# Rows of 309 words instead of 304 under the moving operands of an MLA + mLSTM layer on one Trainium2 core

## The chip, the cores and the metric

One NeuronCore of one Trainium2 chip runs the whole kernel. The metric is the device time of one execution in microseconds. TensorE multiplies matrices, VectorE (DVE), ScalarE (ACT) and GpSimd (POOL) do the rest, and SyncE (SP) issues nearly all loads of weights.

## The reference

One layer of a streaming encoder, for 256 prompt frames, 32 frames of a running stream and 16 learned meta tokens: 304 token columns in all, model width 4096. Cut to what matters here:

```
h = rmsnorm(x) * gain                              # 304 tokens x 4096
p = h @ w_in                                       # latents, mLSTM q, k, v, gates
q = rmsnorm(cq) @ w_q_up ; kv = ckv @ w_kv_up      # cq: 1536 wide, ckv: 512 wide
a = attention(q, kv, kpe) * silu(za)               # 16 heads x 128
m = sigmoid(mo) * rmsnorm(mlstm(q, k, v)) * silu(zb)   # 4 heads x 512
y = x + concat([a, m]) @ w_out                     # 4096 x 4096
```

All inputs and outputs are float32.

## The kernel before

A float32 product is made of three products in the rounded type float32r. Activations and weights are each split into a high part and the remainder, and one 128x128 block of weights times one 128-row block of activations is three matmuls of helper `mm3`: high weights by high activations (L1678), high weights by low activations (L1681), low weights by high activations (L1682). The weights are the stationary operand (128 columns of `whi` or `wlo`), the activations the moving one (`xhi` or `xlo`, 288 or 304 token columns). The result adds up in a PSUM bank over the 32 blocks of the model width.

`group` is the loop of every large projection: for each of the 32 blocks k ("a unit"), for each of four column tiles ct, one `mm3`, so 12 matmuls to a unit. A unit's weights come by DMA as a 128x512 block into `raw`, ScalarE rounds them to `whi` (L727), VectorE takes the remainder to `wlo` (L1132); both have four slots, so the two engines may run three units ahead. `unit_used` counts units that TensorE is done with, and ScalarE waits for it before it overwrites a slot.

The activations stay in SBUF from beginning to end. `xhi` and `xlo` are tiles of 128 partitions by 32 rows of 304 words, one row to each k. The gated mix for the output projection is written over them: before the change, as `mhi` and `mlo`, 32 rows of 288 words that begin where `xhi` and `xlo` begin. Row t of `mhi` is written by ScalarE (`mix`, line 1081) once `unit_used` shows that unit t of the last gate projection is done; VectorE writes `mlo` (line 1622) after it. The latents have tiles of the same sort: `cqhi`, `cqlo` (12 rows of 288 words), `ckhi`, `cklo` (4 rows of 432 words), and are the moving operand of the query and key projections. In the value projection `whi` moves and `ckhi` is stationary.

Where a row begins follows from the sizes of the tiles, which are laid out one behind the other, each start at a multiple of 32 bytes. Counted in bytes modulo 256, the first column that a matmul reads lies here ("place"; for `xhi` with 288 columns it is column 16, with 304 columns it is column 0):

```
tile          start  row step   places of its rows, k = 0, 1, 2, ...   how many
xhi, xlo       192     192      0, 192, 128, 64, 0, ...                  4
mhi, mlo       192     128      192, 64, 192, ...                        2
cqhi, cqlo     192     128      192, 64, 192, ...                        2
ckhi, cklo     192     192      192, 128, 64, 0                          4
whi, wlo       128       0      128 in every slot (512 bytes per column tile)
```

All these are multiples of 64. Small float32r operands lie elsewhere: the rows of `sqr` and `rsr` (squares, high and low parts) begin at place 32 or 160, half way between two multiples of 64; with 288 words they are multiplied by `ones_r` or `blockones_r` in lines 1762, 1858 and 1859. The rows of `ksh`, line 1761, begin at 192 or 64. The plain float32 operand `mqT` of line 2026 begins at 96 or 32.

The program order on each engine is the order of the code; the engines meet at semaphores, and the waits are on constants that `use` works out from a table of phases.

Of the kernel before, what the change touches and what calls it, by code (L numbers as in the profile page):

```python
# [8 lines left out]
SEQ, DEC, PAST, N_META = 256, 32, 128, 16  # L9
# [19 lines left out]
P = 128  # L29
NT = N_META + SEQ + DEC  # L30
NQ = SEQ + DEC
NKV = NT + PAST
C_SAMPLE = N_META + SEQ
KT = D_MODEL // P
KQ = Q_LORA // P
KC = KV_LORA // P
# [13 lines left out]
QT = [(0, 128), (128, 128), (256, 32)]  # L50

MQT = [(0, 112), (112, 128), (240, 48)]

MLW = [(0, 288), (288, 176), (464, 48)]
LAST = NT - 64
# [24 lines left out]
U_OUT = U_GATE + 12 * KT  # L80
# [30 lines left out]
def y_banks(g):  # L111

    return f"out{g}", 4 * (g % 2)
# [14 lines left out]
def use(phase, bank, nth=0, i=0):  # L128

    before, uses = BASE[phase]  # L130
    return before[bank] + nth + i * uses[bank]
# [8 lines left out]
CONST_AT = {}  # L140
# [59 lines left out]
def hymba_step(nc, x_prompt, x_sample, cache_ckv, cache_kpe, state_C, state_n, state_m, meta, norm_gain,  # L200
# [3 lines left out]
    f32, f32r = mybir.dt.float32, mybir.dt.float32r  # L204
# [4 lines left out]
    with ctx:  # L209
        def keep(stack):  # L210
            return lambda name, shape, dt=f32: stack.enter_context(nc.sbuf_tensor(name, shape, dt))

        def sem(name):
            return ctx.enter_context(nc.semaphore(name))
# [6 lines left out]
        con = sb("con", [P, CONST_COLS])  # L221
# [21 lines left out]


        px = ExitStack()
        xhi = keep(px)("xhi", [P, KT, NT], f32r)
        xlo = keep(px)("xlo", [P, KT, NT], f32r)


        p1 = ExitStack()  # L250
# [3 lines left out]

        p2 = ExitStack()
        sb2 = keep(p2)
        cqhi = sb2("cqhi", [P, KQ, NQ], f32r)
        cqlo = sb2("cqlo", [P, KQ, NQ], f32r)
        ckhi = sb2("ckhi", [P, KC, NKV], f32r)
        cklo = sb2("cklo", [P, KC, NKV], f32r)  # L260
        kpe2 = [sb2(f"kpe{h}", [P, NKX]) for h in range(2)]
        qn_ = sb2("qn", [P, SEQ + NQ + WIDE])
        qn = qn_[:, 0:2 * NQ].rearrange("p (h n) -> p h n", h=2)
# [48 lines left out]
        p3 = ExitStack()  # L312
        sb3 = keep(p3)
        hT = sb3("hT", [P, 16, NQ])
        mask = sb3("mask", [P, 512])
        kwh = sb3("kwh", [P, 4, DQK], f32r)
        kwl = sb3("kwl", [P, 2, DQK], f32r)
        vth = sb3("vth", [P, 3, DV], f32r)
# [42 lines left out]
        xres = keep(p4)("xres", [P, 3, 512])  # L361
        p4.close()
        px.close()
        p5 = ExitStack()
        mhi = keep(p5)("mhi", [P, KT, NQ], f32r)
        keep(p5)("meta_gap", [P, KT * N_META])
        mlo = keep(p5)("mlo", [P, KT, NQ], f32r)
        p5.close()

        bank = [ctx.enter_context(nc.psum_tensor(f"bank{b}", [P, 512], f32)) for b in range(8)]  # L370
        full = [sem(f"bank{b}_full") for b in range(8)]
# [47 lines left out]
        mix_hi, mix_lo = sem("mix_hi"), sem("mix_lo")  # L419
# [13 lines left out]
        def _(sp):  # L433
# [36 lines left out]
            for n in range(KT // 2):  # L470
                for b, (a, _) in enumerate(X_BLOCKS):
                    if a == 2 * n * P:
                        x_block(b)
                first_weights(n)
# [231 lines left out]
        def _(act):  # L706
# [265 lines left out]
            def row_hooks(k):  # L972
                if k == 4:

                    act.wait_ge(free[5], use("rows", 5) + 1)
                    act.wait_ge(ml_zero, 1)
                    R = rows
                    nc.scalar.activation(R["mrow"][:, 0:NT], R["xf"][:, 0:NT], ACT.Abs).then_inc(r_abs, 1)
                    act.wait_ge(r_abs, 1)
                    nc.scalar.activation(R["mrow"][:, 0:NT], R["mrow"][:, 0:NT], ACT.Exp, scale=-1.0).then_inc(r_e, 1)  # L980
                    act.wait_ge(r_e, 1)
                    nc.scalar.activation(R["mrow"][:, 0:NT], R["mrow"][:, 0:NT], ACT.Ln, bias=1.0).then_inc(r_l, 1)
                if k == 12:
                    act.wait_ge(r_v, 11)
                    act.wait_ge(full[7], use("rows", 7) + 1)
                    for t, (_, n) in enumerate(MQT):
                        nc.scalar.activation(emcol[0:n, t, :], bank[7][0:n, 4 * t:4 * t + 4], ACT.Exp,
                                             scale=-1.0).then_inc(free[7] if t == 2 else r_em, 1)
# [3 lines left out]
            def mlstm(phase, i, h):  # L992

                def hooks(k):
# [31 lines left out]
                    if k == 17:  # L1026
                        act.wait_ge(din_d, h + 1)
                        for t, (_, n) in enumerate(MQT):
                            b = 5 + t
# [643 lines left out]
        def _(pe):  # L1673
            mm, tr = nc.tensor.matmul, nc.tensor.transpose

            def mm3(out, w_hi, w_lo, m_hi, m_lo, start, stop, opens=False, **kw):

                ins = mm(out, w_hi, m_hi, start=start, stop=False, **kw)  # L1678
                if opens:
                    ins.then_inc(unit_used, 1)  # L1680
                mm(out, w_hi, m_lo, start=False, stop=False, **kw)  # L1681
                return mm(out, w_lo, m_hi, start=False, stop=stop, **kw)  # L1682
# [5 lines left out]
            def fill(phase, b, nth=0, i=0):  # L1688

                before = use(phase, b, nth, i)  # L1690
                if not (isinstance(before, int) and before == 0):
                    pe.wait_ge(free[b], before)
# [12 lines left out]
                ins.then_inc(full[b], 1)  # L1705

            def group(u, phase, nth, i, c0, hooks=lambda k: None, a_hi=xhi, a_lo=xlo, ready=None, x_ready=False,
                      queries=0, b0=0, turn=(0, 2, 1, 3)):

                n = NT - c0  # L1710
                for k in range(KT):
                    pe.wait_ge(lo_done, u + k + 1)
                    if ready is not None:
                        pe.wait_ge(ready, k + 1)
                    if x_ready:
                        pe.wait_ge(free[4 + k % 4], use("x", 4 + k % 4, k // 4) + 1)
                    for ct in range(4) if k else turn:
                        if k == 0:
                            fill(phase, b0 + ct, nth, i)
                        s = slice(ct * P, ct * P + P)  # L1720
                        skip = N_META if ct < queries else 0
                        mc = slice(0, NQ) if a_hi is mhi else slice(c0 + skip, NT)
                        ins = mm3(bank[b0 + ct][:, skip:n], whi[:, k % HL_SLOTS, s], wlo[:, k % HL_SLOTS, s],
                                  a_hi[:, k, mc], a_lo[:, k, mc], k == 0, k == KT - 1, k == 0 and ct == 0)
                        if k == KT - 1:
                            ins.then_inc(full[b0 + ct], 1)
                    if k < KT - 1:
                        ins.then_inc(unit_used, 1)
                    hooks(k)
# [8 lines left out]
            for k in range(X_AHEAD):  # L1738
                x_tile(k)
            warm(WARM[1])  # L1740
            group(0, "cq", 0, 0, N_META, lambda k: x_tile(k + X_AHEAD) if k + X_AHEAD < KT else None, x_ready=True)
            def row_sums(k):
                if k == 6:
# [5 lines left out]
                    ins.then_inc(full[4], 1)  # L1749

            group(KT, "cq", 0, 1, N_META)
            group(2 * KT, "cq", 0, 2, N_META, row_sums)

            def cq_squares(k):
# [221 lines left out]
            def row_hooks(k):  # L1976
# [5 lines left out]
                if k == 9:  # L1982
# [7 lines left out]
                    fill("rows", 7)  # L1990
                    for t, (q0, n) in enumerate(MQT):
                        ins = tr(bank[7][0:n, 4 * t:4 * t + WIDE], rows_["mrow"][0:WIDE, N_META + q0:N_META + q0 + n],
# [4 lines left out]
            def mlstm(phase, i, h):  # L1997
# [3 lines left out]
                def hooks(k):  # L2001
# [36 lines left out]
                    if k == 13:  # L2038
# [8 lines left out]
                        pe.wait_ge(C0_in, 16 * (h + 1))  # L2047
                        for q, (q0, m) in enumerate(MQT):
                            b = 5 + q
# [14 lines left out]
                    if k in (14, 15):  # L2064
                        if k == 14:
                            fill(phase, 4, 2, i)
                        for q, (q0, m) in enumerate(MQT):
                            if (q == 2) != (k == 15):
# [11 lines left out]
                    if k == 23:  # L2080
# [3 lines left out]
                        for e in range(4):  # L2084
                            b = 4 + e
                            fill(phase, b, (3, 2, 3, 3)[e], i)
                            for q, (q0, _) in enumerate(MQT):
                                n = asks[q]
# [43 lines left out]
                group(U_GATE + 2 * KT + g * (2 * KT), "gates", 0, g, N_META)  # L2132

            group(U_GATE + 11 * KT, "gate11", 0, 0, N_META, b0=4)
            group(U_OUT, "out0", 0, 0, N_META, a_hi=mhi, a_lo=mlo, ready=mix_lo)

            def y_rows(g):
                phase, b0 = f"out{g + 1}", y_banks(g)[1]
                for b in range(b0, b0 + 4):
                    pe.wait_ge(free[b], use(phase, b))  # L2140
                for t, (q0, m) in enumerate(QT):
                    for ct in range(4):
                        ins = tr(bank[b0 + t][0:m, ct * P:ct * P + P], yT[:, ct, q0:q0 + m], ident)  # L2143
                    ins.then_inc(full[b0 + t], 1)

            for g in range(1, 8):
                group(U_OUT + g * KT, f"out{g}", 0, 0, N_META, lambda k: y_rows(g - 1) if k == 2 else None,
                      a_hi=mhi, a_lo=mlo, b0=y_banks(g)[1])
            for ct in range(4):
                pe.wait_ge(free[4 + ct], use("out7", 4 + ct) + 1)  # L2150
                for t, (q0, m) in enumerate(QT):
# [168 lines left out]
```

## Time and profile before

| | |
|---|---|
| runs (3) | 2059.68, 2059.81, 2060.38 us; median 2059.81 |
| profiled execution, span from first to last instruction | 2057.9 us |
| TensorE busy | 2046.7 us, 99% |
| VectorE, ScalarE, GpSimd busy | 54%, 44%, 9% |
| HBM traffic | 323.28 MB, 157 GB/s over the span |

For the profiled execution the page gives its span and no other time; the median of the runs is 1.9 us longer than that span. TensorE's matmuls overlap each other in the records, so its busy share says only that it never stood still; how fast it went must be read from the distance between the starts of matmuls. One record of a 288-column float32r matmul lasts about 295 ns, but the next one starts about 133 ns after it.

### The profile page before, as it was taken

Reading aid. Unit: us, or ns where it says so; the run is one execution under the profiler, and the core shown is the slowest. Engines: PE = TensorE matmul, PEld = TensorE weight load, DVE = VectorE, ACT = ScalarE, POOL = GpSimd, SP = SyncE. Lnnn points to the kernel's source line nnn. Section 1 sums busy time; section 2 is a strip of 40 time slices with the busy share of each in tenths; the row PEclk is TensorE's granted clock in tenths of the full one; section 3 lists DMA queues with packets and bytes.
Section 4 is the critical chain, followed back from the end, with each engine's and each line's share of the span. In section 5 each row is a group of like instructions: output and inputs, shape, how many; then the busy total and the mean of one; then the engine's idle time right before and its main releaser. Section 6 shows DMA issues by size and latency. Waiting matters only on the chain.

```text
span 2057.9 us, 36249 instructions
## 1 busy us (share of the span) xinstructions
PE 2046.7 (99%) x15059; PEld 2016.6 (98%) x15059; DVE 1110.8 (54%) x1995; ACT 913.7 (44%) x1826; POOL 180.8 (9%) x206
## 2 busy tenths in 40 slices
PE   9999999999999999999999999999999999999999
PEld 9999999999999999999999999999999999999999
DVE  5545767676555445455555555444555654444444
ACT  5644455565444334343444444444444543333333
POOL 0001033333200000000001011000000000000000
PEclk9999999999999999999999999999999999999999
DMA  9655433333454454645445555555555555555554
GB/s 253 178 171 154 118 118 107 101 100 114 124 170 143 145 163 124 174 123 173 137 142 166 166 169 165 165 167 166 169 164 164 164 185 181 185 187 187 186 182 133
DMA packets 197436, 323.28 MB, mean 157 GB/s; under 512 B 21392, under 2 KB 68136, under 8 KB 197272
## 3 DMA queue, kind: packets, MB, share of 16 engines
q1 hardware_dynamic: 195160, 317.45, 52.1%
q10 hardware_dynamic: 2112, 3.51, 0.5%
q8 instruction: 119, 1.95, 0.4%
q14 instruction: 45, 0.37, 0.1%
HBM read 310.11 MB, written 9.62 MB: 155 GB/s over the span
## 4 chain that ended last, share of the span: by engine, by line
PE 96%; ACT 2%; DVE 1%; issue 1%; DMA 0%; DVEq 0%; ACTq 0%
PE bank L1678 29%; PE bank L1682 29%; PE bank L1681 29%; PE bank L1941 1%; PE bank L1843 1%; PE bank L1840 1%; PE bank L1842 1%; PE bank L1906 1%; PE bank L1907 1%; ACT whi L727 0%; PE bank L2143 0%; PE bank L1703 0%; ACT rsb L819 0%; PE bank L2026 0%; ACT rsb L817 0%
## 5 line engine op out<-in xcount | busy, mean ns | idle before, releaser
L1132 DVE TENSOR_TENSOR wlo<-raw,whi 128x512 fp32r<-128x512 f32 (+1 forms) x1256 | 820.0, 662 | 885.5 <-ACT whi L727 881.9
L727 ACT CAST whi<-raw 128x512 fp32r<-128x512 f32 (+1 forms) x1256 | 708.7, 577 | 980.5 <-PE bank L1682 945.7
L1678 PE MATMUL bank<-xhi,whi 128*128 128x288 f32 (+2 forms) x3104 | 926.7, 299 | 0.0
L1682 PE MATMUL bank<-xhi,wlo 128*128 128x288 f32 (+2 forms) x3104 | 921.8, 297 | 0.0
L1681 PE MATMUL bank<-xlo,whi 128*128 128x288 f32 (+2 forms) x3104 | 921.0, 297 | 0.0
L1678 PEld LDWEIGHTS bank<-xhi,whi 128*128 128x128 f32 (+1 forms) x3104 | 581.7, 187 | 2.0 <-issue 1.1
L1681 PEld LDWEIGHTS bank<-xlo,whi 128*128 128x128 f32 (+1 forms) x3104 | 581.9, 187 | 1.6 <-issue 1.0
L1682 PEld LDWEIGHTS bank<-xhi,wlo 128*128 128x128 f32 (+1 forms) x3104 | 582.0, 188 | 0.0
L1678 PE MATMUL bank<-mhi,whi 128*128 128x288 f32 x1024 | 303.4, 296 | 0.0
L1681 PE MATMUL bank<-mlo,whi 128*128 128x288 f32 x1024 | 302.8, 296 | 0.0
L1682 PE MATMUL bank<-mhi,wlo 128*128 128x288 f32 x1024 | 300.9, 294 | 0.0
L1682 PEld LDWEIGHTS bank<-mhi,wlo 128*128 128x128 f32 x1024 | 192.6, 188 | 0.0
L1681 PEld LDWEIGHTS bank<-mlo,whi 128*128 128x128 f32 x1024 | 192.2, 188 | 0.0
L1678 PEld LDWEIGHTS bank<-mhi,whi 128*128 128x128 f32 x1024 | 192.1, 188 | 0.1
L1678 PE MATMUL bank<-cqhi,whi 128*128 128x288 f32 x288 | 89.5, 311 | 1.2 <-DVE wlo L1132 0.6
L1682 PE MATMUL bank<-cqhi,wlo 128*128 128x288 f32 x288 | 84.8, 295 | 0.0
L1681 PE MATMUL bank<-cqlo,whi 128*128 128x288 f32 x288 | 84.8, 294 | 0.0
L1678 PEld LDWEIGHTS bank<-cqhi,whi 128*128 128x128 f32 x288 | 54.1, 188 | 5.8 <-DVE wlo L1132 3.1
L1681 PEld LDWEIGHTS bank<-cqlo,whi 128*128 128x128 f32 x288 | 54.2, 188 | 0.1
L1682 PEld LDWEIGHTS bank<-cqhi,wlo 128*128 128x128 f32 x288 | 54.1, 188 | 0.0
L2225 POOL TENSOR_SCALAR prob<-prob,pinv 128x144 f32<-128x144 f32 (+2 forms) x48 | 41.7, 883 | 106.4 <-DVE pinv L1354 106.4
L2275 POOL TENSOR_TENSOR attnT<-attnT,gt 128x288 f32<-128x288 f32 x16 | 19.0, 1187 | 198.7 <-DVE gt L1607 198.7
(320 smaller groups left out, 1446.2 us busy)
## 6 DMA issues: line engine op xcount, KB each, us to landing
raw<-in_w_in_dram SPq DMA_DIRECT2D x313, 512.0 KB, 3.8
raw<-in_w_out_dram SPq DMA_DIRECT2D x128, 512.0 KB, 3.7
raw<-in_w_in_dram SPq DMA_DIRECT2D x146, 256.0 KB, 3.0
raw<-in_w_q_up_dram SPq DMA_DIRECT2D x48, 384.0 KB, 3.3
raw<-in_w_kv_up_dram SPq DMA_DIRECT2D x16, 512.0 KB, 3.7
xres<-in_x_prompt_dram SPq DMA_DIRECT2D x16, 256.0 KB, 4.0
out_dram<-ytok SPq DMA_DIRECT2D x15, 256.0 KB, 4.3
xt<-in_x_prompt_dram SPq DMA_DIRECT2D x7, 384.0 KB, 8.3
```

Of the source, the lines that this page charges most:

```text
L727: ins = nc.scalar.copy(hi, src)
L1132: ins = tt(lo, src, hi.bitcast(f32), ALU.subtract)
L1678: ins = mm(out, w_hi, m_hi, start=start, stop=False, **kw)
L1681: mm(out, w_hi, m_lo, start=False, stop=False, **kw)
L1682: return mm(out, w_lo, m_hi, start=False, stop=stop, **kw)
L1840: mm(out, ckhi[:, k, cs], vcols(whi), start=k == 0 and half == 0, stop=False, skip_group_check=True)
L1842: mm(out, cklo[:, k, cs], vcols(whi), start=False, stop=False, skip_group_check=True)
L1843: ins = mm(out, ckhi[:, k, cs], vcols(wlo), start=False, stop=last, skip_group_check=True)
L1906: mm(out, qn[:, h, q0:q0 + P], kn[:, h, 0:keys], start=True, stop=False)
L1907: ins = mm(out, qpm[h][:, q0:q0 + P], kpe2[h][:, 0:keys], start=False, stop=True)
L1941: ins = mm(bank[5][:, q0:q0 + w], vt[:, t, vh], probT[:, at:at + w], start=t == 0, stop=t == 3, skip_group_check=True)
L2225: ts_(prob[0:n, at:at + w], prob[0:n, at:at + w], pinv[0:n, t:t + 1], None, ALU.mult).then_inc(pn, 1)
```

## The change

The rows of `xhi` and `xlo` become 309 words, those of `cqhi` and `cqlo` 293, those of `ckhi` and `cklo` 437: five unused words behind each. A gap of 32 words is put ahead of `xhi`, one of 16 words ahead of `cqhi`. `mhi` and `mlo` are no tiles of their own any more but the columns 16 to 303 of `xhi` and `xlo`, so each mixed row takes the place of the activation row of the same number. To pay for the space, the 128x512 mask of the mLSTM loses its tile and is loaded over the cosine and sine tables, at the same point of the DMA queue, behind the same waits.

```
+X_ROW = 309
+Q_ROW = 293
+CK_ROW = 437
+ROW_GAP = 32
+LATENT_GAP = 16
...
-        xhi = keep(px)("xhi", [P, KT, NT], f32r)
-        xlo = keep(px)("xlo", [P, KT, NT], f32r)
+        keep(px)("row_gap", [P, ROW_GAP])
+        xhi_ = keep(px)("xhi", [P, KT, X_ROW], f32r)
+        xlo_ = keep(px)("xlo", [P, KT, X_ROW], f32r)
+        xhi, xlo = xhi_[:, :, 0:NT], xlo_[:, :, 0:NT]
+        mhi, mlo = xhi_[:, :, N_META:NT], xlo_[:, :, N_META:NT]
+        mask = con[:, CONST_AT["cos"][0]:CONST_AT["cos"][0] + 512]
...
-        cqhi = sb2("cqhi", [P, KQ, NQ], f32r)
-        cqlo = sb2("cqlo", [P, KQ, NQ], f32r)
-        ckhi = sb2("ckhi", [P, KC, NKV], f32r)
-        cklo = sb2("cklo", [P, KC, NKV], f32r)
+        sb2("latent_gap", [P, LATENT_GAP])
+        cqhi = sb2("cqhi", [P, KQ, Q_ROW], f32r)[:, :, 0:NQ]
+        cqlo = sb2("cqlo", [P, KQ, Q_ROW], f32r)[:, :, 0:NQ]
+        ckhi = sb2("ckhi", [P, KC, CK_ROW], f32r)[:, :, 0:NKV]
+        cklo = sb2("cklo", [P, KC, CK_ROW], f32r)[:, :, 0:NKV]
...
-        mask = sb3("mask", [P, 512])
...
-        p5 = ExitStack()
-        mhi = keep(p5)("mhi", [P, KT, NQ], f32r)
-        keep(p5)("meta_gap", [P, KT * N_META])
-        mlo = keep(p5)("mlo", [P, KT, NQ], f32r)
-        p5.close()
...
-                        mc = slice(0, NQ) if a_hi is mhi else slice(c0 + skip, NT)
+                        mc = slice(0, NQ) if mixed else slice(c0 + skip, NT)
```

The places after it, for the first column that is read:

```
tile           first place   row step   places
xhi, 288 cols     128          212      32 different multiples of 4 (128, 84, 40, 252, ...)
xlo, 288 cols       0          212      32 different multiples of 4 (0, 212, 168, 124, ...)
mhi, mlo          as xhi and xlo with 288 columns
cqhi              128          148      12 different multiples of 4
cqlo              128          148      12 different multiples of 4
ckhi, cklo     128, 224        212      4 each
whi, wlo        128 as before
```

Of every four neighbouring rows, one begins at a multiple of 16 bytes and three do not. The number, the kind, the shape and the order of the instructions are the same on all five engines (14,589 rows of TensorE, 805 of ScalarE, 1,028 of VectorE, 128 of GpSimd and 239 of SyncE stand in the same order as before); only the names of the mask and of the mixed operands differ. No wait is added, removed or moved. Tiles behind `xhi` shift by 32 words and more, and most of them keep a start at a multiple of 32 bytes: `sqr` goes to place 160, `rsr` to 32.

## Rows read from the trace of the kernel before

**Rows 1.** The page: span, busy time (us, share, instructions) and granted clock.

```profile
span 2057.9 us, 36249 instructions
...
PE 2046.7 (99%) x15059; PEld 2016.6 (98%) x15059; DVE 1110.8 (54%) x1995; ACT 913.7 (44%) x1826; POOL 180.8 (9%) x206
...
PEclk9999999999999999999999999999999999999999
```

**Rows 2.** The page: chain that ended last, shares by engine and line.

```profile
PE 96%; ACT 2%; DVE 1%; issue 1%; DMA 0%; DVEq 0%; ACTq 0%
PE bank L1678 29%; PE bank L1682 29%; PE bank L1681 29%; PE bank L1941 1%; PE bank L1843 1%; PE bank L1840 1%; PE bank L1842 1%; PE bank L1906 1%; PE bank L1907 1%; ACT whi L727 0%; PE bank L2143 0%; PE bank L1703 0%; ACT rsb L819 0%; PE bank L2026 0%; ACT rsb L817 0%
```

**Rows 3.** Waits of TensorE alone: us in total, times, longest.

```profile
PE bank L1735 <- DMA con<-in_shape_table_dram: 4.2, 1, 4.2
PE bank L2036 <- DVE kwh L1522: 1.4, 4, 0.3
PE bank L1678 <- DVE wlo L1132: 0.6, 1, 0.6
```

**Rows 4.** Waits of all compute engines: us in total, times, longest.

```profile
ACT whi L727 <- PE bank L1682: 945.7, 915, 6.7
DVE wlo L1132 <- ACT whi L727: 881.9, 902, 6.6
```

**Rows 5.** Stretches, all engines: from:to, length, busy us (instructions), PEclk, DMA, GB/s.

```profile
1078.00:1634.90 556.90, 556.90 (x4210) 556.90 (x4209) 292.40 (x436) 237.26 (x409) 46.81 (x44) 1.00 0.57 166
1635.10:2052.00 416.90, 416.90 (x3157) 416.56 (x3156) 203.35 (x314) 168.72 (x289) 3.82 (x4) 1.00 0.55 178
```

**Rows 6.** Chain in order of time: start us, us, one set of 12 transposes.

```profile
1691.05 1.31 PE bank L2143 x12
```

**Rows 7.** Groups by line and shape, TensorE: count, busy us, mean ns of one.

```profile
L1678 PE MATMUL bank<-xhi,whi 128*128 128x288 f32 x2176 | 647.1, 297 | 0.0
L1681 PE MATMUL bank<-xlo,whi 128*128 128x288 f32 x2176 | 641.8, 295 | 0.0
L1682 PE MATMUL bank<-xhi,wlo 128*128 128x288 f32 x2176 | 641.7, 295 | 0.0
L1678 PE MATMUL bank<-mhi,whi 128*128 128x288 f32 x1024 | 303.4, 296 | 0.0
L1681 PE MATMUL bank<-mlo,whi 128*128 128x288 f32 x1024 | 302.8, 296 | 0.0
L1682 PE MATMUL bank<-mhi,wlo 128*128 128x288 f32 x1024 | 300.9, 294 | 0.0
...
L1681 PE MATMUL bank<-xlo,whi 128*128 128x304 f32 x896 | 269.6, 301 | 0.0
```

**Rows 8.** Groups by shape, TensorE: a plain float32 matmul.

```profile
L2026 PE MATMUL bank<-mqT,mkT 128*128 128x288 f32 x16 | 4.5, 405 | 0.0
```

**Rows 9.** Order of time, gate projections: start us, us; units begin at five.

```profile
1501.69 0.29 PE L1678 MATMUL bank<-xhi,whi 128*128 128x288 f32 x1
...
1503.29 0.29 PE L1678 MATMUL bank<-xhi,whi 128*128 128x288 f32 x1
...
1504.87 0.29 PE L1678 MATMUL bank<-xhi,whi 128*128 128x288 f32 x1
...
1505.80 0.29 PE L1681 MATMUL bank<-xlo,whi 128*128 128x288 f32 x1
1505.92 0.29 PE L1682 MATMUL bank<-xhi,wlo 128*128 128x288 f32 x1
1506.06 0.30 PE L1678 MATMUL bank<-xhi,whi 128*128 128x288 f32 x1
...
1506.45 0.30 PE L1678 MATMUL bank<-xhi,whi 128*128 128x288 f32 x1
...
1508.05 0.29 PE L1678 MATMUL bank<-xhi,whi 128*128 128x288 f32 x1
```

**Rows 10.** Order of time, output projection: first matmul of three units.

```profile
1866.60 0.30 PE L1678 MATMUL bank<-mhi,whi 128*128 128x288 f32 x1
...
1868.18 0.29 PE L1678 MATMUL bank<-mhi,whi 128*128 128x288 f32 x1
...
1869.79 0.30 PE L1678 MATMUL bank<-mhi,whi 128*128 128x288 f32 x1
```

**Rows 11.** Groups by shape, TensorE: small float32r matmuls on `sqr`, `rsr`, `ksh`.

```profile
L1859 PE MATMUL bank<-sqr,ones_r 128*128 128x288 f32 x16 | 4.5, 295 | 0.0
L1858 PE MATMUL bank<-rsr,ones_r 128*128 128x288 f32 x16 | 4.4, 292 | 0.0
...
L1761 PE MATMUL bank<-ksh,ones_r 128*128 128x288 f32 x12 | 3.6, 296 | 0.0
L1762 PE MATMUL bank<-sqr,ones_r 128*128 128x288 f32 x12 | 3.5, 294 | 0.0
```

More of the change, by code:

```diff
@@ L1707, in group @@
             def group(u, phase, nth, i, c0, hooks=lambda k: None, a_hi=xhi, a_lo=xlo, ready=None, x_ready=False,
-                      queries=0, b0=0, turn=(0, 2, 1, 3)):
+                      queries=0, b0=0, turn=(0, 2, 1, 3), mixed=False):
                 n = NT - c0
@@ L2134, in _ @@
             group(U_GATE + 11 * KT, "gate11", 0, 0, N_META, b0=4)
-            group(U_OUT, "out0", 0, 0, N_META, a_hi=mhi, a_lo=mlo, ready=mix_lo)
+            group(U_OUT, "out0", 0, 0, N_META, a_hi=mhi, a_lo=mlo, mixed=True, ready=mix_lo)
             def y_rows(g):
@@ L2147, in _ @@
                 group(U_OUT + g * KT, f"out{g}", 0, 0, N_META, lambda k: y_rows(g - 1) if k == 2 else None,
-                      a_hi=mhi, a_lo=mlo, b0=y_banks(g)[1])
+                      a_hi=mhi, a_lo=mlo, mixed=True, b0=y_banks(g)[1])
             for ct in range(4):
```

## The prediction

> **What bounds the kernel now.** I read the page's head first: TensorE is busy 2046.7 of 2057.9 us, with the granted clock at nine tenths or more, in every slice [rows 1]. The chain of work that ended last is 96% TensorE, and 87% lies on the three lines of `mm3` [rows 2]. The waits of TensorE come to 6.2 us, 4.2 of which are the first load [rows 3]. The suppliers wait for TensorE and not the reverse: ScalarE stood 945.7 us before its casts because a slot was still in use, VectorE 881.9 us behind ScalarE [rows 4]. So no engine, queue or transfer but TensorE decides the time, and only the distance between the starts of its matmuls can move it.
>
> How large is that distance? The two long stretches without other work give it. From 1078 to 1634.9 us TensorE starts 4210 matmuls in 556.9 us, 132.3 ns each; from 1635.1 to 2052 us 3157 in 416.9 us, of which 84 are transposes [rows 5]; the granted clock is 1.00 in both. A set of 12 transposes takes 1.31 us [rows 6], seven sets 9.2, so 3073 matmuls are left with 407.7 us, 132.7 ns each. The records last 294 to 297 ns [rows 7], about 163 ns more than the distance; this remainder is the latency of one matmul, hidden by the next. So I use the mean of a form, less 163, as its distance, and trust differences between forms to about 1 ns.
>
> A plain float32 matmul of 288 columns lasts 405 ns [rows 8]: distance 242, and it takes the columns twice, so 121 ns for one pass. The same columns in float32r cost 133 in one pass. About 12 ns of each of the 13,440 big matmuls (3104, 1024, 288 and 64 `mm3`) are therefore not arithmetic. Something about fetching the moving words at full rate costs it, and that is what the place of a tile could touch.
>
> It does depend on the place. In the gate projections the units start at 1501.69, 1503.29, 1504.87, 1506.45 and 1508.05 us [rows 9]: 1.60, 1.58, 1.58 and 1.60 us for 12 equal matmuls, at the places 0, 192, 128 and 64 in this order. In the output projection a unit takes 1.58 us at place 192 and 1.61 at 64 [rows 10]. So two of the four places cost 133.3 ns a matmul and the two others 131.7, a difference of 1.6 ns or 1.2%, with the same weights' place and the same shapes.
>
> **The change part by part.** Removed and added instructions: none. The order is the same on all engines, the mask's load stands where it stood, and a mixed row is written behind the same count of units, so no wait grows. These edits cost nothing, covered by the 945.7 us that ScalarE idles; were that cover gone, one mixed row costs a cast of about 0.6 us on an engine that is 44% busy [rows 1], still not on the path. The unused words are never read or loaded.
>
> What is left is the price of 13,440 matmuls at other places. No row of the trace has a moving tile of that size that begins off a multiple of 32 bytes, so this price must be bounded.
>
> From below: if spreading the tiles removed all the 12 ns, every matmul would go at the float32 pass's 121 ns, 13,440 x 12 = 161 us, giving 1899 us. I see nothing that says so; even the best place keeps 10 to 11 of the 12 ns.
>
> From above: 16 more words in a row (304 instead of 288) cost 301 - 295 = 6 ns [rows 7]. A tile that begins inside a piece touches one piece more at its end. If pieces were 64 bytes, all but 2 of 32 rows would pay 6 ns, 13,440 x 6 x 0.94 = 76 us and 2136 us. But the rows that begin at 32 or 160 would pay it too, and they do not (next paragraph). With pieces of 32 bytes the price is 3 ns for seven rows of eight, 35 us, 2095 us; the trace has no such row and can't exclude it. With pieces of 16 bytes it is 1.5 ns for three rows of four, 15 us, 2075 us.
>
> The nearest rows: float32r, 288 columns, half way between multiples of 64. `rsr` by `ones_r` 292 ns, `sqr` by `ones_r` 295 (16 of each), and in the other place of the code 294 for `sqr` beside 296 for `ksh`, which lies at a multiple of 64 [rows 11]. The mean over the 44 is (16 x 292 + 16 x 295 + 12 x 294)/44 = 293.6; the big forms have 295.5 [rows 7]. So off the multiples of 64 a matmul is 1 to 2 ns cheaper, like the better pair of places. I take the smaller half of it, since these matmuls have other neighbours and only two places: 1.2 ns less for each of the 13,440, 16 us.
>
> The sum: 2057.9 - 16.1 = 2041.8 us of span, plus 1.9 us around it, **2044 us**, 0.8% faster. By the better pair of places alone it would be about the same: (1.60 - 1.58)/12/2 = 0.8 ns, 11 us, 2049 us.
>
> The trace shows by itself that distances vary with the start. The Trainium skill ("SBUF — State Buffer", Specifications (TRN2)) says that SBUF is read in lines of 16 bytes and that each crossing into a new line costs a penalty. By it a row of 288 words that begins off a multiple of 16 bytes crosses one line more, which speaks against this change and is the third rival below; its own sum there is 2075 us where mine is 2044. No run here shows a tile off 16 bytes, so the trace neither confirms nor refutes it.
>
> **The rivals.**
>
> *Much faster* (chance 0.13). The 12 ns come from two streams, moving words and the next weights, that meet at a common grid of 64 bytes. All big rows and all weights lie on it now. Off the grid they would slip past each other and a third or more of the 12 ns goes: from 4 ns, 54 us, 2006 us. For it: the price depends on the place at all, and identical matmuls in one unit differ (1505.80, 1505.92 and 1506.06 us begin three neighbours [rows 9]). Against: the rows half way between, which are off this grid, keep 10 of the 12 ns.
>
> *No change* (0.16). The four places now average 132.5 ns, and 32 places average the same, because what is lost is lost on the average over all phases. Between 2056 and 2064 us. For it: the gate stretch with four places and the output stretch with two differ by only 0.4 ns. Against: the rows at 32 and 160.
>
> *Slower by the partial piece* (0.34). A tile that begins inside a 16-byte piece costs one more, as worked out above: +15 us, 2075 us; with pieces of 32 bytes +35 us, 2095 us. It decides as soon as a tile off 16 bytes costs over 0.4 ns more than one on it, on the average (0.4 x 3/4 x 13,440 = 4 us), with no gain at the others. For it: the moving stream seems to have no slack, since at half the rate (plain float32) the 12 ns vanish altogether, and a stream without slack pays for each additional fetch. Against: nothing that was measured off 16 bytes, and a 32-byte offset cost nothing.
>
> A transfer or a supplier that becomes the bound is excluded: the stretches move 166 and 178 GB/s [rows 5], which a gain of 0.8% raises to 167 and 179, with both producers idle for about half of the time.
>
> **How the numbers follow.** Small gain 0.37 (2030 to 2054), much faster 0.13, no change 0.16, slower 0.34, of which some 0.26 by the 16-byte piece (2064 to 2085) and 0.08 by more. The forecast is that of the likeliest, 2044 us. Faster by over 0.2% 0.50, within 0.2% 0.16, slower 0.34; 0.2% (4 us) is about what a measurement of this kernel can tell from none. The range for 8 in 10 reaches from the middle of the much faster case to just past the 16-byte case, 2008 to 2086 us, and leaves out half of the first and the larger pieces of the last. The likeliest case's own range is 2030 to 2054.
>
> **What the profile after would show.** The count of records (15,059) and the granted clock stay. The means of the three lines fall from about 295 to 294 ns for 288 columns. The gate stretch, 4210 matmuls in 556.9 us, takes 552, and the output stretch 416.9 us becomes 413. Units no longer alternate between two lengths with a period of four but wander over 32. If the partial piece is real, units whose row begins off 16 bytes take 1.60 to 1.62 us and every fourth one stays at 1.58 to 1.60. If the grid matters, units at places 0, 64, 128 and 192 are the long ones and most others are below 1.56. TensorE's waits stay at 6 us; if they grew, the argument that nothing else bounds would be wrong, and so would the forecast.

## The result, and the profile after

The changed kernel takes 2072.35 us (2072.11 to 2073.46, 4 runs), the kernel before 2059.74 us (2059.46 to 2060.38, 4 runs) beside it: a ratio of 1.0061, interval 1.0049 to 1.0073. It is slower by 12.6 us, and the forecast was 2044 us.

The page of the changed kernel begins so (share of the span and instructions as before):

```profile
span 2070.3 us, 36249 instructions
...
PE 2059.9 (99%) x15059; PEld 2030.0 (98%) x15059; DVE 1109.2 (54%) x1995; ACT 913.7 (44%) x1826; POOL 180.2 (9%) x206
...
PEclk9999999999999999999999999999999999999999
```

The same 15,059 matmuls at the same granted clock keep TensorE busy 13.2 us longer; VectorE, ScalarE and GpSimd are where they were in [rows 1]. The waits of TensorE in the changed kernel:

```profile
PE bank L1740 <- DMA con<-in_shape_table_dram: 4.1, 1, 4.1
PE bank L1683 <- DVE wlo L1137: 0.7, 2, 0.6
PE bank L2041 <- DVE kwh L1527: 0.3, 1, 0.3
```

They are 5.1 us against 6.2 in [rows 3]. So nothing waits more. The matmuls themselves stand further apart. One stretch of the gate projections, the same for all kernels below, shows it (from:to, length, busy us and count of each engine, clock, DMA share, GB/s). First the kernel before, then the changed one:

```profile
1110.00:1630.00 520.00, 520.00 (x3931) 520.00 (x3930) 272.22 (x408) 221.96 (x384) 42.06 (x40) 1.00 0.58 166
```

```profile
1110.00:1630.00 520.00, 520.00 (x3899) 520.00 (x3898) 270.26 (x405) 219.90 (x381) 42.07 (x40) 1.00 0.58 165
```

520 us over 3931 are 132.3 ns for each, over 3899 they are 133.4. I call this quotient the distance from here on; it is the number by which the experiments are read. 1.1 ns times 13,440 matmuls is 14.8 us, somewhat more than the 12.4 us between the spans. The output projection lost less (2651 records before and 2641 after in 350 us from 1701 us on, 132.0 and 132.5 ns): before the change its rows lay at two places only, while the first experiment below, aligned rows with the mix in place, has 2660 records there, 131.6 ns.

The groups of the changed kernel by line and shape, against [rows 7], where the big forms had 294 to 297 ns and 301 for 304 columns:

```profile
L1683 PE MATMUL bank<-xhi,whi 128*128 128x288 f32 x3200 | 954.2, 298 | 0.2 <-DVE wlo L1137 0.2
L1686 PE MATMUL bank<-xlo,whi 128*128 128x288 f32 x3200 | 949.1, 297 | 0.0
L1687 PE MATMUL bank<-xhi,wlo 128*128 128x288 f32 x3200 | 948.2, 296 | 0.0
...
L1686 PE MATMUL bank<-xlo,whi 128*128 128x304 f32 x896 | 271.5, 303 | 0.0
```

And where the time sits is seen unit by unit. In the changed kernel, in order of time, five neighbouring units of a gate projection begin with these rows; the rows of `xhi` that they read begin at the places 112, 68, 24, 236 and 192 modulo 256, which is 0, 4, 8, 12 and 0 modulo 16:

```profile
1510.94 0.29 PE L1683 MATMUL bank<-xhi,whi 128*128 128x288 f32 x1
...
1512.53 0.30 PE L1683 MATMUL bank<-xhi,whi 128*128 128x288 f32 x1
...
1514.17 0.30 PE L1683 MATMUL bank<-xhi,whi 128*128 128x288 f32 x1
...
1515.77 0.29 PE L1683 MATMUL bank<-xhi,whi 128*128 128x288 f32 x1
...
1517.35 0.29 PE L1683 MATMUL bank<-xhi,whi 128*128 128x288 f32 x1
```

12 matmuls take 1.59 us at 0 modulo 16, 1.64 at 4, 1.60 at 8 and 1.58 at 12. In [rows 9] no unit took over 1.60. Taken over the whole trace (each 288-column matmul's start to the next start, from the order of time, grouped by where its moving row begins modulo 16; pairs with another kind of work between them left out):

```
place modulo 16      0       4       8       12
changed kernel     132.4   135.7   134.2   131.5 ns   (2,580 to 2,594 each)
kernel before      132.5     -       -       -        (10,334)
```

So on the average the price goes by the start within 16 bytes, and it has both signs: a row at 4 or 8 is dear, one at 12 is cheaper than an aligned one. Modulo 64 the classes at 12 bytes lie close together (12, 28, 44 and 60: 131.2, 131.8, 131.5 and 131.4 ns), those at 4 bytes less so (4, 20, 36 and 52: 136.7, 135.9, 135.1 and 135.1 ns). The start within 16 bytes is therefore not all that counts; the section on two columns less comes back to this.

### The profile page after: what moved, and what is told of

Same layout as the page of the kernel before. It is cut to its first block, busy times and chain, and to the rows that moved or that the text cites. A ratio compares the mean times of both kernels' runs of the same rounds, so it can differ in the third digit from the quotient of the medians.

```text
span 2070.3 us, 36249 instructions
## 1 busy us (share of the span) xinstructions
PE 2059.9 (99%) x15059; PEld 2030.0 (98%) x15059; DVE 1109.2 (54%) x1995; ACT 913.7 (44%) x1826; POOL 180.2 (9%) x206
## 4 chain that ended last, share of the span: by engine, by line
PE 97%; ACT 1%; DVE 1%; DMA 0%; issue 0%; SPq 0%; DVEq 0%; ACTq 0%
PE bank L1683 30%; PE bank L1686 29%; PE bank L1687 29%; PE bank L1946 1%; PE bank L1848 1%; PE bank L1845 1%; PE bank L1847 1%; PE bank L1911 1%; PE bank L1912 1%; PE bank L2148 0%; PE bank L1708 0%; ACT rsb L824 0%; PE bank L2031 0%; ACT rsb L822 0%; PE bank L2067 0%; ACT whi L732 0%
## 5 line engine op out<-in xcount | busy, mean ns | idle before, releaser
L1683 PE MATMUL bank<-xhi,whi 128*128 128x288 f32 (+2 forms) x4128 | 1236.1, 299 | 0.2 <-DVE wlo L1137 0.2
L1686 PE MATMUL bank<-xlo,whi 128*128 128x288 f32 (+2 forms) x4128 | 1230.2, 298 | 0.0
L1687 PE MATMUL bank<-xhi,wlo 128*128 128x288 f32 (+2 forms) x4128 | 1229.2, 298 | 0.0
L1683 PEld LDWEIGHTS bank<-xhi,whi 128*128 128x128 f32 (+1 forms) x4128 | 778.8, 189 | 2.5 <-issue 1.1
L1686 PEld LDWEIGHTS bank<-xlo,whi 128*128 128x128 f32 (+1 forms) x4128 | 778.4, 189 | 1.6 <-issue 1.0
L1687 PEld LDWEIGHTS bank<-xhi,wlo 128*128 128x128 f32 (+1 forms) x4128 | 779.2, 189 | 0.0
L1845 PE MATMUL bank<-whi,ckhi 128*128 128x256 f32 x128 | 36.0, 281 | 0.0
L1848 PE MATMUL bank<-wlo,ckhi 128*128 128x256 f32 x128 | 36.0, 281 | 0.0
L1847 PE MATMUL bank<-whi,cklo 128*128 128x256 f32 x128 | 36.0, 281 | 0.0
L822 ACT ACTIVATE rsb<-bank,epsc 128x288 f32<-128x288 f32 (+2 forms) x42 | 22.5, 537 | 21.9 <-DVE qn L1307 21.4
L2280 POOL TENSOR_TENSOR hT<-hT,sg 128x288 f32<-128x288 f32 x16 | 14.2, 921 | 185.7 <-ACT sg L1069 185.7
```

The source lines that it names most:

```text
L822: nc.scalar.activation(dst, src, ACT.Ln, scale=scale, bias=epsc[:, :]).then_inc(free[bank_no], 1)
L1845: mm(out, ckhi[:, k, cs], vcols(whi), start=k == 0 and half == 0, stop=False, skip_group_check=True)
L1847: mm(out, cklo[:, k, cs], vcols(whi), start=False, stop=False, skip_group_check=True)
L1848: ins = mm(out, ckhi[:, k, cs], vcols(wlo), start=False, stop=last, skip_group_check=True)
L2280: tt(dst[:, ds(at + ct, 1), :], dst[:, ds(at + ct, 1), :], src[:, ct:ct + 1, :], ALU.mult)\
```

## The experiments

All but one of the kernels below use rows of 304, 288 and 432 words again, and all keep the mix in place and the mask over the tables.

### The change without its rows

```
-X_ROW = 309
-Q_ROW = 293
-CK_ROW = 437
-ROW_GAP = 32
-LATENT_GAP = 16
+X_ROW = 304
+Q_ROW = 288
+CK_ROW = 432
```

> The changed kernel with rows of 304, 288 and 432 words again and no gaps: the mix stays in place and the mask stays over the tables. Theory A (what costs is where a tile begins and ends inside a 16-byte piece): 2060 us, as before, since all places are multiples of 64 again; 2058 to 2062. Rival B (the mix in place or the mask's new place costs something): 2072 us.

2058.19 us, ratio 0.9993 (0.9983 to 1.0002): the mix in place and the mask's new place cost nothing, and the rows carry the whole loss. This kernel differs from the changed one in the rows alone, and against it the change costs 14.2 us, close to the 14.8 us worked out above. Its stretch has as many records as that of the kernel before:

```profile
1110.00:1630.00 520.00, 520.00 (x3931) 520.00 (x3930) 271.99 (x408) 221.84 (x384) 42.10 (x40) 1.00 0.58 166
```

### Spread, but on multiples of 16 bytes

```
-X_ROW = 309
-Q_ROW = 293
-CK_ROW = 437
+X_ROW = 308
+Q_ROW = 292
+CK_ROW = 436
```

> Rows of 308, 292 and 436 words with the gaps of the change: the tiles are spread over 16 places modulo 256, all multiples of 16. Theory A: no tile begins inside a piece, so 2056 to 2061 us (in the trace of the changed kernel the matmuls at multiples of 16 start 132.4 ns apart, before all of them 132.5). Rival C (spreading the rows over many places itself costs): about as the change, 2068 to 2074 us.

2061.26 us, ratio 1.0007 (0.9998 to 1.0016), and 3925 records, 132.5 ns:

```profile
1110.00:1630.00 520.00, 520.00 (x3925) 520.00 (x3924) 271.90 (x407) 221.40 (x383) 42.15 (x40) 1.00 0.58 166
```

Against the kernel before, the spread over many places makes no difference that is clear of the noise. Against the kernel of the first experiment, which differs in the row lengths and gaps alone and ran beside it, it costs about 3 us (2060.76 to 2062.40 against 2057.85 to 2059.69, 10 runs each). So of the 14.2 us that the rows cost, 11.1 are taken away by one word less in the row, and about 3 stay with the spread rows of 308 words.

### One residue at a time

Each tile gets room for a shift, and all rows begin 1, 2 or 3 words later; here for three words:

```
+def shifted(tile, off, rows, row):
+    return tile[:, off:off + rows * row].rearrange("p (k n) -> p k n", k=rows)
...
-xhi_ = keep(px)("xhi", [P, KT, X_ROW], f32r)
+xhi_ = shifted(keep(px)("xhi", [P, KT * X_ROW + 64], f32r), 3, KT, X_ROW)
```

and the same for `xlo`, `cqhi`, `cqlo`, `ckhi` and `cklo`.

> Rows of 304, 288 and 432 words, all moved by one word, so that every row begins 4 bytes behind a multiple of 64 and there are only four places. Theory A: the changed kernel's matmuls at 4 modulo 16 start 135.7 ns apart, 3.2 more than before, times 13,440 is 43 us: 2095 to 2110 us. Rival C (only the spread matters): 2060 us. A rule by which each tile off 16 bytes costs the same 4/3 of the change's 12.6 us: 2077 us.

> Every row 8 bytes behind a multiple of 64, rows of 304, 288 and 432 words. Theory A, by the changed kernel's matmuls at 8 modulo 16 (134.2 ns apart): 134.2 ns in the gate stretch, 2078 to 2086 us. A price that is the same for all tiles off 16 bytes is out already (4 bytes 2099 us, 12 bytes 2051 us).

> As the run before it, but moved by three words, so that every row begins 12 bytes behind a multiple of 64. Theory A with a cost that depends on which words of the piece are used (12 modulo 16 start 131.5 ns apart in the changed kernel, 1.0 less than before): 2043 to 2052 us, faster than both kernels. A rule by which each tile off 16 bytes costs the same: 2077 us. Rival C: 2060 us.

One word: 2099.08 us, ratio 1.0190 (1.0173 to 1.0207). Two words: 2084.51 us in one run, beside 2059.37 before. Three words: 2051.17 us, ratio 0.9957 (0.9942 to 0.9972). The stretches, in this order:

```profile
1110.00:1630.00 520.00, 520.00 (x3843) 520.00 (x3842) 263.58 (x393) 214.55 (x369) 42.11 (x40) 1.00 0.57 162
```

```profile
1110.00:1630.00 520.00, 520.00 (x3878) 520.00 (x3877) 268.33 (x402) 218.56 (x379) 42.14 (x40) 1.00 0.58 164
```

```profile
1110.00:1630.00 520.00, 520.00 (x3947) 520.00 (x3947) 273.38 (x411) 221.65 (x385) 42.07 (x40) 1.00 0.58 167
```

Distances of 135.3, 134.1 and 131.7 ns. Together with the 132.3 of the aligned rows their mean is 133.4 ns, the changed kernel's own distance (133.4): it is a mixture of the four residues (the starts modulo 16 bytes) in equal parts. The shift by three words beats both kernels: by 8.6 us the kernel before (the 131.5 ns read in the changed kernel had promised 13), and by 7.0 us the same kernel with aligned rows.

### Weights shifted too

```
-whi = sb("whi", [P, HL_SLOTS, 512], f32r)
-wlo = sb("wlo", [P, HL_SLOTS, 512], f32r)
+whi = shifted(sb("whi", [P, HL_SLOTS * 512 + 64], f32r), 1, HL_SLOTS, 512)
+wlo = shifted(sb("wlo", [P, HL_SLOTS * 512 + 64], f32r), 1, HL_SLOTS, 512)
```

on top of the kernel in which all rows begin one word late.

> Every row of the moving tiles and of the weights, whi and wlo, 4 bytes behind its old place, so that the two lie to each other as in the kernel with rows of 304 words. Theory A (the moving tile's own pieces decide): as with the moving tiles alone, 135.4 ns in the gate stretch, 2095 to 2103 us. Rival D (two streams collide by their distance modulo 64 or 256 bytes): 132.4 ns, 2058 us.

2102.26 us in one run, 135.5 ns:

```profile
1110.00:1630.00 520.00, 520.00 (x3839) 520.00 (x3838) 261.99 (x389) 214.54 (x367) 42.06 (x40) 1.00 0.57 161
```

Moving both leaves the mean price about where it was (135.3 ns and 2099.08 us with the moving tiles alone); it does not bring back the 132.3 ns of rival D, which had the two at their old distance. The idea behind the "much faster" rival, that off the common grid of 64 bytes at least 4 ns go, is refuted by the three kernels before this one: with the weights on the grid and the moving rows 4, 8 or 12 bytes off it, the best gain is 0.6 ns. The weights' place is not without effect, though. Taken apart by row number modulo 4, the units of the gate stretch stand at 135.8, 134.0, 136.3 and 135.6 ns with the moving tiles alone, and at 134.6, 135.6, 134.7 and 137.4 ns with both. Weights shifted alone were not tried.

### Two columns less

`group` leaves out the last two token columns in the gate and output projections, so their values there are not computed; an odd number of columns was not tried. The edit takes two columns from the moving tile and from the PSUM output alike. It reaches 7,680 matmuls (the records of 286 columns), not the 7,296 of the first expectation.

```
+less = 2 if phase[:4] in ("gate", "out0", "out1", ..., "out7") else 0
+mc = slice(mc.start, mc.stop - less)
-ins = mm3(bank[b0 + ct][:, skip:n], ...
+ins = mm3(bank[b0 + ct][:, skip:n - less], ...
```

> Rows of 304 words at multiples of 64, and the 7,296 matmuls of the gate and output projections leave out the last two token columns (286 of 288): they begin on a multiple of 16 bytes and end in the middle of a piece. By columns alone the distance falls by 0.8 ns to 131.5. Theory A1 (words of the last piece that go unused are paid): it stays at 132.2 to 132.5. Theory A2 (the price lies in the first piece): 131.5.

> Every row 8 bytes behind a multiple of 64 and 286 columns in the gate and output projections: these matmuls begin in the middle of a piece and end at the end of one. Theory A1 (the last piece is paid): 131.5 to 132.5 ns in the gate stretch, although the 288-column matmuls of the same kernel cost 134.2. Theory A2 (the first piece is paid): 133.4.

> Every row 4 bytes behind a multiple of 64, and 286 columns in the gate and output projections: such a tile begins with 3 words of its first 16-byte piece and ends with 3 of its last, 72 pieces in all. Theory A3 (what counts is how many pieces a tile touches: 72 here, 73 with 288 columns): 131.4 ns in the gate stretch, as the two other 286-column kernels, 2060 to 2070 us. Theory A4 (a start at 4 bytes is dear by itself): 134.6 ns, 2093 us.

> Every row 12 bytes behind a multiple of 64, and 286 columns in the gate and output projections: one word in the first piece, one in the last, 73 pieces. Theory A3 (number of pieces): dearer than the other 286-column kernels, 132.5 to 133.5 ns in the gate stretch. Theory A4 (a start at 12 bytes is cheap by itself): 130.8 to 131.2.

The stretches with shifts of 0, 2, 1 and 3 words, in the order of the expectations (2050.88, 2061.46, 2081.16 and 2054.60 us, one run each; the shift still has its price in the other 5,760 of the 13,440 matmuls, so the times are not compared):

```profile
1110.00:1630.00 520.00, 520.00 (x3960) 520.00 (x3959) 273.59 (x411) 222.97 (x386) 42.10 (x40) 1.00 0.59 167
```

```profile
1110.00:1630.00 520.00, 520.00 (x3960) 520.00 (x3959) 273.49 (x411) 223.42 (x386) 42.18 (x40) 1.00 0.59 167
```

```profile
1110.00:1630.00 520.00, 520.00 (x3911) 520.00 (x3910) 270.25 (x404) 220.57 (x381) 42.13 (x40) 1.00 0.58 165
```

```profile
1110.00:1630.00 520.00, 520.00 (x3939) 520.00 (x3938) 272.67 (x409) 222.03 (x385) 42.11 (x40) 1.00 0.58 167
```

In one table, with the words that a tile uses of its first and its last piece of 16 bytes, the pieces it touches, and the distance less that of the columns alone (0.42 ns each, by the 121 ns of [rows 8] for 288 columns):

```
columns  place  first/last  pieces  distance  less columns
288        0      4 / 4       72      132.3      11.3
288        4      3 / 1       73      135.3      14.3
288        8      2 / 2       73      134.1      13.1
288       12      1 / 3       73      131.7      10.7
286        0      4 / 2       72      131.3      11.1
286        8      2 / 4       72      131.3      11.1
286        4      3 / 3       72      133.0      12.8
286       12      1 / 1       73      132.0      11.8
```

Neither A1 (the last piece is paid) nor A2 (the first is paid) survives the pair 286 at 0 and at 8: with a full first and half a last piece, or the other way round, the matmul costs the same in the mean, and about as much as two full ones. But a half at both ends (288 at 8) costs 2 ns more, which fits A3, the count of pieces. A3 in turn fails at the odd places: 286 at 4 touches only 72 pieces and costs 1.7 ns more than the other two with 72. A4 was off by as much at this place (134.6 expected, 133.0 measured), and at 12 bytes, where it had 130.8 to 131.2, 132.0 was measured. By the last column, a start at 4 costs 2.5 ns more than a start at 12 where the last piece has 1 word, and 2.1 ns more where it has 3; a last piece of 1 word costs 1.5 or 1.1 ns more than one of 3. So both ends matter. I found no rule of one number that gives all eight.

And these eight are means over rows at four places modulo 256. Taken apart by the row number k modulo 4, from each matmul's start to the next in the same stretch, they read:

```
columns  place   k mod 4:  0       1       2       3
288        0             133.3   131.7   131.3   133.2 ns
288        4             135.8   134.0   136.3   135.6
288        8             135.1   133.5   134.4   133.6
288       12             131.8   133.2   131.3   131.0
286        0             132.4   131.7   133.3   128.1
286        8             132.3   130.6   129.5   133.1
286        4             133.5   132.1   133.5   133.1
286       12             132.6   132.8   131.2   131.7
```

In the kernel with 286 columns at place 0, the units that begin with these records, at k = 14, 15 and 16, take 1.60, 1.54 and 1.59 us:

```profile
1500.64 0.30 PE L1684 MATMUL bank<-xhi,whi 128*128 128x286 f32 x1
...
1502.24 0.30 PE L1684 MATMUL bank<-xhi,whi 128*128 128x286 f32 x1
...
1503.78 0.30 PE L1684 MATMUL bank<-xhi,whi 128*128 128x286 f32 x1
...
1505.37 0.29 PE L1684 MATMUL bank<-xhi,whi 128*128 128x286 f32 x1
```

The pattern is no noise: the kernel before and the kernel with aligned rows of 304 words have the same four numbers to 0.1 ns. So within one residue the rows differ by 1.4 to 5.3 ns, as much as the residues differ in the mean. The equal means of 286 at 0 and at 8 are made of unequal units, and the cheap start at 12 is cheap in the mean but not at every row (133.2 against 131.7 ns at k = 1 modulo 4). What decides this is open. In these kernels k modulo 4 gives the row's place modulo 256 and the weights' slot at once. The kernel with rows of 308 words parts them: with k a multiple of 4, so always in slot 0, its rows at the places 0, 64, 128 and 192 stand at 132.0, 132.3, 133.6 and 133.3 ns over the whole trace, so it is not the slot alone; and place 0 in slot 0 has 133.3 ns in the kernel before, so it is not place and slot together either. The neighbouring rows differ between the two kernels.

### High parts at 4, low parts at 12

The shift is 1 word for `xhi`, `cqhi`, `ckhi` and 3 for `xlo`, `cqlo`, `cklo`, with all columns.

> All 288 or more columns; the high parts 4 bytes behind a multiple of 64, the low parts 12 bytes behind one. If a tile's own place sets the distance to the next start, the distance is about 135.4 ns after a matmul on high parts and 131.8 after one on low parts, 134.2 in the mean, 2085 us. If the tile that follows sets it, 131.8 ns before a low and 135.4 before a high. If the seam of both counts (how full the last piece of the one and the first of the other are), high to high stays at 135.4 and the two others differ from both numbers.

2079.36 us in one run:

```profile
1110.00:1630.00 520.00, 520.00 (x3886) 520.00 (x3885) 269.34 (x404) 219.73 (x380) 42.07 (x40) 1.00 0.58 164
```

133.8 ns; the mean of two thirds at 4 and one third at 12 would be 134.1. By the order of time (288 columns, start to next start, over the whole trace) a high row followed by a high one is at 134.0 ns, high to low at 133.1 and low to high at 134.6. In the kernel with all rows at 4 the same three are 137.0, 134.6 and 134.7. So neither a tile's own place nor its follower's sets a distance alone, and even the pair doesn't: high to high has the same places in both kernels and differs by 3 ns. The third expectation, the seam, had that one unchanged, so it fails as well. I take from it that a single start-to-start distance can't be read as one matmul's price, and go by the sum over many.

## Why the prediction was wrong

**The bound held.** No engine, queue or wait but TensorE's own pace moved: 13.2 us more busy time of TensorE, 5.1 us of waits, clock 1.00 in the stretch. The edits costed at nothing cost nothing (ratio 0.9993 without the rows).

**The step that failed** is the nearest row. I took `sqr` and `rsr`, at the places 32 and 160, for tiles "off the grid", read 1 to 2 ns less from them than from the big forms, and put 1.2 ns less for each of the 13,440 matmuls into the sum. In its place the runs showed 1.1 ns more in the stretch (133.4 against 132.3). Both places are multiples of 16, so they said nothing of a tile that is not. And the gain itself was no property of the half-way place. The trace of the kernel before has two more groups on the same two tiles, with `blockones_r` as the other operand, which the mean of 293.6 ns leaves out:

```profile
L1859 PE MATMUL bank<-sqr,blockones_r 128*128 128x288 f32 x8 | 2.4, 297 | 0.0
L1858 PE MATMUL bank<-rsr,blockones_r 128*128 128x288 f32 x8 | 2.4, 296 | 0.0
```

They are as dear as the big forms (294 to 297 ns), and with them the mean over all 60 is 294.4 ns. In the changed kernel the two tiles lie 128 bytes further, `sqr` at 160 and `rsr` at 32, still half way, and their groups read:

```profile
L1863 PE MATMUL bank<-rsr,ones_r 128*128 128x288 f32 x16 | 4.5, 298 | 0.0
L1864 PE MATMUL bank<-sqr,ones_r 128*128 128x288 f32 x16 | 4.5, 296 | 0.0
```

298 and 296 ns where [rows 11] had 292 and 295, while the two groups with `blockones_r` read 294 and 293 there instead of 296 and 297. The reading of `rsr` moved by 6 ns when the tile moved by 128 bytes, more than the effect I read from it. The 16 places of the kernel with 308 words, all multiples of 16, are at 132.5 ns: spreading aligned tiles gains nothing (it costs 0.2 ns against the aligned rows of 304 words), which is about what the rival "no change" said of them.

The bound from below, 121 ns for the columns alone, rested on plain float32 taking the columns twice, and that holds: by start to next start in the trace before, plain float32 costs 79.7 ns for 96 columns more (162.3 ns at 192 columns, 242.0 at 288), 0.83 ns each, and float32r 62.9 ns for 144 more (132.5 at 288, 195.4 at 432), 0.44 ns each.

**The rival that happened** is the slower one, with pieces of 16 bytes: 15 us were worked out, 12.6 measured, 2075 against 2072.35 us. Its average was right, 1.5 ns for each tile off 16 bytes by the forecast and (135.3 + 134.1 + 131.7)/3 - 132.3 = 1.4 ns measured. Its picture of one equal extra piece is wrong: 3.0, 1.8 and -0.6 ns by residue. That the average of such unlike numbers came out at 1.4 is in part luck, and with it the time of 2075 us. The units that it put at 1.58 to 1.60 us (on 16 bytes) and 1.60 to 1.62 (off it) came out as 1.59, and 1.64, 1.60 and 1.58. Its deciding point, 0.4 ns, was passed by 1.0.

The Trainium skill's rule ("SBUF — State Buffer", Specifications (TRN2)), of a penalty for each crossing into a new 16-byte line, agrees with the period of 16 bytes and with the sign of the mean. It does not give the cheap start at 12 bytes (one line more than aligned, and 0.6 ns less), nor the dear 286 columns at 4 bytes (as many lines as aligned, and 1.7 ns more). There the measurement decides.

**The chances.** The Trainium skill's rule and the lack of slack were both in the text as reasons for the slower case, and against it stood only "a 32-byte offset cost nothing", which is no argument about pieces of 16. With it left out, the slower case should have had most of the chance.

**Left open.** Why three words late is cheaper and one word late dearer than aligned, and why rows of one residue differ as they do. For the means, the runs exclude the distance from the weights modulo 64 as the sole cause (both shifted by 4 bytes: 135.5 against 135.3 ns), the first piece alone, the last piece alone and the count of pieces alone. Not separated are the end of the moving tile and the end of the PSUM output, and what the neighbouring rows do. Fetching words in pairs would single out the odd places, but it was not tested and would not tell 4 from 12.

## What to carry to other kernels

Where a matmul's moving operand is float32r at full rate, keep its rows on the same place within 16 bytes: a row of an odd number of words puts three rows of four off it, and here the mean lost 1.1 ns in 132. If rows can't be aligned, or one has a word to spend, look at each residue apart, since the mean over residues hides a cheap one (here three words late: ratio 0.9957), and time the whole kernel, since rows of one residue differ too. And price an unknown place only from rows that have the property in question, in number, and not from a few small matmuls whose place differs in some other way; where the trace has more groups on the same tile, read them all.

## What was not expected of the hardware

A start 12 bytes into a 16-byte piece is, in the mean, faster than an aligned start: 131.7 against 132.3 ns over some 3,940 matmuls, and 2051.17 us for the kernel against 2058.19 with aligned rows and 2059.82 before. Two columns less are worth 1.0 ns on aligned rows, 2.8 ns at 8 bytes, 2.3 at 4, and cost 0.3 ns at 12. Of plain float32 the runs say nothing: the tiles of [rows 8] still begin at a multiple of 32 bytes in the changed kernel (406 ns against 405).
